# Output projection's second weight block split ahead of the squares, and three small products one step later in a two-block transformer kernel

## What is computed

```python
def first_block(x, g_pre_mix, g_post_mix, w_qkv, w_o, rel_bias, g_pre_ffn, g_post_ffn, w_gate, w_up, w_down):
    for i in range(DEPTH):
        h = rms_norm(x, g_pre_mix[i])
        if i % N_MIXERS == 0:
            m = chunk_relpos_attention(h, w_qkv[i], w_o[i], rel_bias[i // N_MIXERS])
...
        x = x + rms_norm(m, g_post_mix[i])
        h = rms_norm(x, g_pre_ffn[i])
        x = x + rms_norm(swiglu(h, w_gate[i], w_up[i], w_down[i]), g_post_ffn[i])
    return x

def chunked_spatial_gating(u, v, ln_g, ln_b, w_s, b_s):
    bsz, s, _ = v.shape
    v = layer_norm(v, ln_g, ln_b)
    vc = v.reshape(bsz, s // GM_CHUNK, GM_CHUNK, GM_GROUPS, GM_GROUP_DIM)
...
    mixed = jnp.einsum('gts,bcsge->bctge', w, vc) + jnp.transpose(b_s)[None, None, :, :, None]
    return u * mixed.reshape(bsz, s, W)
...
        dots = jnp.einsum('bqhd,bsd->bqhs', qib, k_idx).astype(jnp.float32) * (IDX_DIM ** -0.5)
        score = jnp.einsum('bqh,bqhs->bqs', wib.astype(jnp.float32), jax.nn.relu(dots))
```

## Time and profile before

| | us |
|---|---|
| median of 3 runs | 1278.51 |
| lowest and highest | 1278.12 to 1279.11 |
| the profiled execution: time | 1278.12 |
| the profiled execution: span | 1276.0 |
| TensorE busy in it | 1267.5 (99%) |
| VectorE busy | 762.3 (60%) |
| ScalarE busy | 594.4 (47%) |
| GpSimd busy | 40.3 (3%) |

### The profile page before, as it was taken

One profiled execution on the slowest core, in us unless ns is written; L12 is line 12 of the kernel. 1 busy time (PEld: TensorE's weight loads), 2 busy tenths in 40 slices (PEclk: granted clock), 3 DMA queues, 4 the chain that ended last, 5 costly groups with the idle time before them and its releaser, 6 DMA issues.

```text
span 1276.0 us, 16938 instructions
## 1 busy us (share of the span) xinstructions
PE 1267.5 (99%) x6329; PEld 1058.7 (83%) x6329; DVE 762.3 (60%) x1555; ACT 594.4 (47%) x1240; POOL 40.3 (3%) x79
## 2 busy tenths in 40 slices
PE   9999999999999999999999999999999999999998
PEld 7888777898888888888888888888878788999987
DVE  5367775754555446447574677775545534976664
ACT  5367665543453345335553334663335543463633
POOL 1000000100000000001100000000000000000000
PEclk9999999999999999999999999999999999999999
DMA  7243442126552646232523232112221025758431
GB/s 249 100 146 111 132 124 84 67 99 188 137 147 90 202 128 198 82 117 99 194 71 116 99 132 99 34 67 99 99 99 67 33 99 173 190 153 228 132 133 66
DMA packets 28481, 155.84 MB, mean 122 GB/s; under 512 B 3560, under 2 KB 3820, under 8 KB 12400
## 3 DMA queue, kind: packets, MB, share of 16 engines
q1 hardware_dynamic: 23208, 132.80, 29.7%
q0 software_dynamic: 2304, 16.78, 6.9%
q10 hardware_dynamic: 2888, 5.18, 1.3%
HBM read 146.35 MB, written 4.20 MB: 118 GB/s over the span
## 4 chain that ended last, share of the span: by engine, by line
PE 96%; DVE 1%; issue 1%; DMA 0%; ACT 0%; POOL 0%; SPq 0%; ACTq 0%; POOLq 0%; DVEq 0%
PE bank L2071 26%; PE bank L2073 26%; PE bank L2072 26%; PE sc L2242 3%; PE tp L2251 2%; PE ob L2308 1%; PE ob L2266 1%; PE sc L2073 1%; PE sc L2072 1%; PE sc L2071 1%; PE bank L2176 1%; PE bank L2186 1%; PE bank L2193 1%; DMA w_raw<-in_weights 0%; PE ob L2073 0%
## 5 line engine op out<-in xcount | busy, mean ns | idle before, releaser
L2071 PE MATMUL bank<-xT_hi,w_hi 128*128 128x512 f32 (+1 forms) x1040 | 407.0, 391 | 0.1
L2073 PE MATMUL bank<-xT_hi,w_lo 128*128 128x512 f32 (+1 forms) x1040 | 395.6, 380 | 0.0
L2072 PE MATMUL bank<-xT_lo,w_hi 128*128 128x512 f32 (+1 forms) x1040 | 395.1, 380 | 0.0
L1283 DVE TENSOR_TENSOR w_lo<-w_raw,w_hi 128x512 fp32r<-128x512 f32 x404 | 257.5, 686 | 140.2 <-ACT w_hi L730 138.6
L730 ACT ACTIVATE w_hi<-w_raw 128x512 fp32r<-128x512 f32 x404 | 226.7, 621 | 78.0 <-PE bank L2073 67.7
L2071 PEld LDWEIGHTS bank<-xT_hi,w_hi 128*128 128x128 f32 x1040 | 195.8, 188 | 39.4 <-issue 4.5
L2073 PEld LDWEIGHTS bank<-xT_hi,w_lo 128*128 128x128 f32 x1040 | 195.6, 188 | 37.9
L2072 PEld LDWEIGHTS bank<-xT_lo,w_hi 128*128 128x128 f32 x1040 | 196.1, 189 | 34.9 <-issue 1.2
L738 ACT ACTIVATE arena<-bank 128x512 f32<-128x512 f32 x74 | 43.8, 597 | 137.8 <-PE bank L2073 132.6
L2071 PE MATMUL bank<-w_hi,act_hi 128*128 128x512 f32 (+1 forms) x264 | 102.7, 389 | 0.0
L2073 PE MATMUL bank<-w_hi,act_lo 128*128 128x512 f32 (+1 forms) x264 | 101.2, 383 | 0.0
(11 more groups left out here) (284 smaller groups left out, 1773.9 us busy)
## 6 DMA issues: line engine op xcount, KB each, us to landing
w_raw<-in_weights SPq DMA_DIRECT2D x99, 1024.0 KB, 4.9
arena<-in_weights POOLq DMA_DIRECT2D x16, 1024.0 KB, 9.2
arena<-in_weights SPq DMA_DIRECT2D x9, 1024.0 KB, 8.3
arena<-in_bias ACTq DMA_DIRECT2D x16, 256.0 KB, 2.9
act_lo<-act_lo SPq DMA_DIRECT2D x24, 128.0 KB, 2.6
x_sb<-in_x SPq DMA_DIRECT2D x4, 512.0 KB, 6.6
w_raw<-in_weights SPq DMA_DIRECT2D x4, 512.0 KB, 8.1
x_dram<-x_sb SPq DMA_DIRECT2D x1, 2048.0 KB, 12.3
```

The source lines that it names most:

```text
L1283: nc.vector.tensor_tensor(w_lo[SPLIT_AT[b]][:, cols], w_raw[SLOT[b]][:, cols], w_hi[SPLIT_AT[b]][:, cols].bitcast(F32), ALU.subtract).then ...
L2071: nc.tensor.matmul(ps, hi_l, hi_r, start=first, stop=False, skip_group_check=onto)
L2072: nc.tensor.matmul(ps, hi_l, lo_r, start=False, stop=False, skip_group_check=onto)
L2073: return nc.tensor.matmul(ps, lo_l, hi_r, start=False, stop=last, skip_group_check=onto)
```

## The change

Two edits. On ScalarE and VectorE the split of wo1's second weight block (FIRST["wo0"] + 3) is written ahead of the squares and gains of wo0, no longer behind them. And in SMALL_AT three entries of TensorE's table are one step k larger: of block 0, chunk 0, the first (1 to 2); of block 0, chunk 1, the second (3 to 4); of block 1, chunk 0, the third (6 to 7).

```diff
-SMALL_AT = (((1, 3, 4, 6, 7), (1, 3, 5, 7)), ((0, 3, 6), (0, 4)), ((0, 4), (0, 4)), ((), ()))
+SMALL_AT = (((2, 3, 4, 6, 7), (1, 4, 5, 7)), ((0, 3, 7), (0, 4)), ((0, 4), (0, 4)), ((), ()))
...
             step(parts, PARTS)
+            split(FIRST["wo0"] + 3)
             for t in range(TT):
                 act.wait_ge(bank_full, USE["wo0"] + t + 1)
                 sum_squares("post1a", t, bank[(USE["wo0"] + t) % 4][:, :])
-            split(FIRST["wo0"] + 3)
...
             step(parts, PARTS)
+            split(FIRST["wo0"] + 3)
             for t in range(TT):
                 begin_variance("post1", t)
                 gain_wo(0, t)
-            split(FIRST["wo0"] + 3)
             norms(1, m_sb, lambda t: None, lambda t: gain_wo(1, t), FIRST["wo1"] + 2, FIRST["wo1"] + 3)
```

## The result

The changed kernel takes 1282.86 us in the median of 7 runs (1282.55 to 1284.10), the kernel before 1278.36 us (7 runs, 1278.12 to 1279.35). The ratio is 1.0036, with a 95% interval of 1.0026 to 1.0046: slower by 4.5 us. Forecast were 3.0 us more, in a range that reached to 1283.6.

The account below looks back on a forecast made before the run. TensorE's stream of matmuls plus a few short gaps was taken as the bound. The late wo1 start, +4.0 us, and the three moved products, -1.0 us, gave +3.0 us: 1281.5 us, range 1280.2 to 1283.6.

Parts of the forecast that it names:

- main case: Whole kernel: late wo1 start less the small products' gain, +3.0 us, ends +2.5 and +3.4; chance 0.67.
- clock rival: At wo1's start: TensorE's clock halves after the idle gap, costing 1.3 to 1.7 us more, 1282.8 to 1283.2; chance 0.20.
- The late start of wo1: Before wo1's first matmul: the split's wait and work delay bank 0, start 228.82 instead of 224.62, 4.20 us late.
- its three values: TensorE's start lag behind a VectorE result: 0.05, 0.15 and 0.26 us; the middle one was taken.
- The table moves: At three mixing and indexer products: later places close gaps of 0.73 us plus restarts, -1.0 us, ends 0.7 and 1.1.
- the third mixing product: Possible new wait for the first mixing product's bank, met or missed by under 0.1 us; nothing taken for it.
- The 0.30 us of the second block: At wo1's second weight block: the early split removes a 0.19 us gap and 0.11 us restart, winning 0.30 us.
- Nothing given back: Behind wo1's late start: the chain of waits through the norms moves as a whole, so no delay is recovered.
- The sum without the clock: Whole kernel: +4.0 us at wo1 less 1.0 us at the small products, +3.0 us.
- no gap opens: At wo1's start: the split's wait is met early, so both edits gain, 1.3 us less, 1277.2 us; chance 0.05.
- the moves win nothing: At the small products: each wait moves with its product, so +4.0 us stands alone, 1282.5 us; chance 0.08.
- the gap is only 3.5 us: At wo1's start: split and squares overlap better, net under 2.6 us, 1280.5 to 1281.0 us; chance 0.11.

Follow-up runs that it names:

- the filled gap: Changed kernel with 16 extra unread 128x512 matmuls on TensorE ahead of wo1, in the wait for bank 0: 1281.14 us, ratio 1.0023.
- two quarters: Changed kernel with only two of the split's four quarters ahead of the squares, the other two behind them: 1281.52 us, ratio 1.0023.
- the last experiment: Kernel before with the three table entries moved and the split put between tiles 0, 1 and tiles 2, 3: 1276.82 us, ratio 0.999.
- the first experiment: Kernel before with only the three table entries moved, the split still behind the squares: 1277.20 us, ratio 0.9993.

## Why the prediction was right, and where it fell short

The direction, the place and the size of the late start came as forecast. The size of the whole did not: 4.5 us more instead of 3.0, above the main case's own end of 3.4. The measured time lies in the range because the range took in most of the clock rival, and that rival is what happened on top.

- **The late start of wo1.** Forecast were 4.20 us, from 224.62 to 228.82; measured are 4.13 (the last matmul of wo0 starts at 224.47 here, so 224.70 was due, and 228.83 is the start). The steps held one by one: VectorE's split, and not the square, sets the gain's start (the square ends at 227.05 + 0.58, the gain starts at 228.09), and the lag from VectorE to TensorE was 228.83 - (228.09 + 0.68) = 0.06 us, at the short end of its three values.
- **The clock.** This is the term that was mis-sized: the likeliest case had it at nothing, and gave the rival with it a chance of 0.20 and a price of 1.3 to 1.7 us. It came: even the fastest of the seven runs is 1.0 us above 1281.5. Its price is the difference to the filled gap, 4.5 - 2.9 = 1.6 us in the median, and 2.8 us in the profiled execution. That the median falls into the rival's 1.3 to 1.7 is in part luck: that price was read from slow products at the start of the program, and the traces have 2.8 us here and 1.6 us behind two quarters. The step that failed is the sentence that "the gap is only just the longest", by which the term stayed out of the sum. With 4.0 us against the 1.6 us of the earlier trace rows it was two and a half times as long, outside everything that the trace could speak for, and the row that came nearest, the half pace behind idle time at the start, spoke rather for a slow stretch. (It does not show the clock: the granted clock reads 1.00 there, and no run tells what made those products slow.) The rule of the Trainium skill, "TensorE: Matmul & The Clock Gate", section "Why this matters for your kernels", advises against such gaps, since the array is throttled behind them. The trace agrees with it at 4.0 us (granted clock 0.53 in the stage behind).
- **The table moves.** Forecast -1.0, measured -1.0 in the runs and between two marks of the trace. All three gaps are closed, and the third mixing product met its bank: VectorE emptied it at 658.51 + 0.69 = 659.20, TensorE came at 659.41.
- **The 0.30 us of the second block.** The gap is gone where the split is early. By the difference of the last experiment to the table moves alone it was worth 0.4 us.
- **Nothing given back.** The sum without the clock, +3.0, was measured as +2.9 with the gap filled; the chain of norms behind it moved as a whole: VectorE's quarter at 254.62 starts at 261.55 in the changed kernel, 6.9 us later, and the marks at 648 us are 6.96 us later.
- **The other rivals.** That no gap opens fell with the trace, that the moves win nothing with the first experiment, and that the gap is only 3.5 us with the 3.97 us of the trace.

## What to carry to other kernels

When an instruction is moved ahead in a queue, its wait moves too: ask what event it waits for, and when the instructions that are now behind it could have run. Here a split that could not start before the last bank was full was put ahead of the work that frees the first bank, to save 0.3 us, and made TensorE 4.1 us late; put where its wait is just about met, it wins what there was to win (0.4 us). And an idle stretch on TensorE is to be priced with what follows it: the same matmuls may then run at half the clock for a while.

## What the runs showed of the hardware

The granted clock stayed full behind an idle stretch of 1.6 us (1.00 in the profile; ten runs within 0.35 us, with mean granted clocks of 0.999 to 1.0). Behind 2.8 us it fell in the profiled execution (0.59 in the stage), and nine of ten runs have the time that goes with a fall. Behind 4.0 us it fell in the profiled executions of both kernels that have this stretch, and by time and mean granted clock in every run of the changed kernel. A time alone is weaker evidence than a trace: one of 19 runs of the kernel before took 1280.73 us, with a mean granted clock of 0.998, and nothing tells why.

What the fall costs varied from one execution to the next, with the same idle stretch. In the profiled run of the changed kernel the clock fell 3.3 us into the stretch, and the matmuls were slow up to 234.97; with the split alone it fell 2.1 us into it, and they were back at 0.23 us apart soon after 233.57. So the length of the idle stretch by itself does not tell when the clock falls, nor how many matmuls then run slowly: they lost 2.8 us in the one and 2.2 us in the other (eleven intervals, 228.71 to 233.57, where 2.6 us were due). The rest of what decides it no run shows. The runs of the changed kernel lie over 1.5 us. Sixteen matmuls that compute nothing of use, put into the stretch, took away the cost, and nine of ten runs then lay within 0.25 us.
